# The modulation product of a three-layer kernel, moved from TensorE's gaps to POOL during the gate and up products

## The chip, the core and the metric

The kernel runs on one core of a Trainium2 chip. It is one launch, and the metric is the device time of that launch in microseconds (us). Engines are named as in the profile: PE (TensorE, matmul), PEld (its weight loads), DVE (VectorE), ACT (ScalarE), POOL (GpSimd), SP (SyncE, which only issues transfers here). Each has its own instruction stream, and they meet at semaphores. SBUF is the on-chip memory of 128 partitions, PSUM the banks that matmuls write.

## What is computed

Two hybrid layers (first block), then one layer of a second block. Only the second block has a conditioning vector c, and its modulation is a function of c and of weights alone:

```python
def hybrid_layer(x, ...):                      # called twice
    h = _rms(x) * norm1_g
    proj = h @ w_in
    ...
    o_a = sliding_window_attention(...) @ w_attn_o
    o_b = rwkv7_time_mix(...) @ w_rwkv_o
    o_c = retention(...) @ w_ret_o
    mixed = g[:, :, 0] * o_a + g[:, :, 1] * o_b + g[:, :, 2] * o_c
    x = x + mixed @ w_out
    h2 = _rms(x) * norm2_g
    x = x + (jax.nn.silu(h2 @ w_ffn_gate) * (h2 @ w_ffn_up)) @ w_ffn_down
    return x
# second block: modulation = c @ w_ada + b_ada, (1, 1024) @ (1024, 6144), six vectors of 1024
```

Sizes: 256 tokens, width 1024, hidden width 2816, fp32 throughout. `w_ada` is 25 MB.

## The kernel before

The streams are written out by hand, with no scheduler: what stands in a row in an engine's function is what that engine executes in order. Weights come in slots of 4096 floats a partition through a ring of three (`ring`, SP issues a slot's two transfers of 1 MB as soon as the blocks that read the slot three back are done). PE works in numbered blocks; `Q_...` are block numbers, `S_...` slot numbers, `block_done` counts finished blocks, and `dve_taken` and `act_taken` count the PSUM banks that were emptied.

Most products are split in two parts for precision. ACT copies a weight slot rounded (`high_weights`, L2459), DVE subtracts the copy from the slot (`low_weights`, L2723), and PE multiplies both parts. In the feed-forward part (`ffn`), a slot holds a gate and an up tile of 256 columns; eleven slots follow each other. For a slot, DVE adds the halves of the gate tile (L3139) and the up tile (L3148) from PSUM, multiplies with the silu (L3154), rounds the product (L2751), takes the remainder (L2754), and then makes the low part of the slot two further on (L2723). Block `Q_DOWN`, the first of eight of the down product, follows the last slot.

The modulation product stands in the first block. Each layer handles half of `w_ada`, as six slots of 2 MB (`S_ADA`) in the same ring. `ada(l, n)` on PE multiplies one slot with c: eight matmuls in the code, whose output is 32 partitions wide so that four lie beside each other in the array (L1884). c is a column of `cond`, with zeros around, so that each slot's sum lands in a partition of its own. DVE adds the six results (`ada_rows`, L2918 and L2921) and `ada_columns` turns the sums into columns with four small matmuls (L1893), which DVE adds to the bias in `mod` (L2926).

These six products stand where PE would wait for another engine: one ahead of the two merging levels of the RWKV solve (`rwkv_levels`), two in chunk 0, two in chunk 1 (`rwkv_chunk`), one in the norm and retention part. In the levels, four more gaps hold the four blocks of the first branch's output product (`mix(l, 0, ...)`, L1902), one whole block of 16 recorded matmuls each.

POOL does little: it fills with zeros, multiplies by the cosine table (L1850) and by the retention gate (L1852), and at the layer's end clears semaphores and passes `layer_go` on.

Of the kernel before, what the change touches and what calls it, by code (L numbers as in the profile page):

```python
# [68 lines left out]
LAYER_SLOTS, TWO_SLOTS, EXPERT_SLOTS = 45, 12, 12  # L69
# [12 lines left out]
S_ADA, S_MIX, S_OUT, S_FFN, S_DOWN = [15, 17, 18, 19, 20, 21], [16, 22, 23], 24, 26, 37  # L82
# [3 lines left out]
for _s, _q in list(zip(S_ADA, Q_ADA)) + [(_s, _q[-1]) for _s, _q in zip(S_MIX, Q_MIX)]:  # L86
    SLOT_DONE[_s] = _q + 1
# [178 lines left out]
def build(nc, io):  # L266

    ctx = ExitStack()
    with ctx:
# [30 lines left out]
        mod = sb("mod", [P, 48])  # L300
        bias = sb("bias", [P, 4])
# [116 lines left out]
        mod_rows = w_(15360, 512)  # L418
# [14 lines left out]
        group_sums, group_taken = sem("group_sums"), sem("group_taken")  # L433

# [1344 lines left out]
        def _(sp):  # L1779
# [15 lines left out]
            for l in range(LAYERS):  # L1795
                for n in range(LAYER_SLOTS):
# [32 lines left out]
        def _(pool):  # L1829
            pool.memset(bias[:, 0:1], EPS).then_inc(bias_set, 1)  # L1830
            pool.memset(bias[:, 1:2], LNX_EPS).then_inc(bias_set, 1)
            pool.memset(bias[:, 2:3], 1.0).then_inc(bias_set, 1)
            for l in range(LAYERS):
# [22 lines left out]
                pool.sem_inc(layer_go, 1)  # L1856
            second_pool(pool)

        @block.tensor
        def _(pe):  # L1860
# [15 lines left out]
            def ada(l, n):  # L1876


                q, s = Q_ADA[n], S_ADA[n] % RING
                pe.wait_ge(ring_full[s], full(l, S_ADA[n]))  # L1880
                taken(l, q)
                for k in range(KD):
                    j = 32 * (k % 4)
                    mm = nt.matmul(PS[j:j + 32, bank(l, q), :], cond[:, k, 32 - n:64 - n], ring[:, s, 512 * k:512 * (k + 1)],  # L1884
                                   start=(k < 4), stop=(k >= 4))
                mm.then_inc(block_done, 1)

            def ada_columns(l):

                taken(l, Q_COLS)  # L1890
                pe.wait_ge(dve_taken, taken_at(l, Q_ADA[-1]))
# [1373 lines left out]
```

## Time and profile before

| what | value |
| --- | --- |
| time, median of three runs | 2178.12 us (2176.33 to 2178.39) |
| time of the profiled execution | 2175.79 us |
| its span | 2173.9 us |
| PE busy | 1803.5 us, 83% of the span |
| DVE busy | 941.3 us, 43% |
| ACT busy | 556.0 us, 26% |
| POOL busy | 30.2 us, 1%, 23 instructions |

Times within a trace are in us from the span's start. Layer 0 runs from 0 to about 530 us, layer 1 to about 1040, the second block's mixers to about 1290, and the experts to the end. The profiled execution is 1.9 us longer than its span, and 2.3 us shorter than the median.

### The profile page before, as it was taken

The numbers are of one execution on the slowest core, as the hardware profiler recorded it, in microseconds if no ns is written. First come the engines' busy times: TensorE is split into PE (matmuls) and PEld (weight loads), VectorE is DVE, ScalarE is ACT, GpSimd is POOL, SyncE is SP. The second block draws the span as 40 slices with busy tenths as digits, with TensorE's granted clock in tenths as the row PEclk, the third lists the DMA queues.
The fourth block names the chain that finished last, engine by engine and source line by source line (L and its number), as shares of the span: only waits on it lengthen the run. The fifth ranks groups of instructions, "written<-read, shape, count | busy, mean of one in ns | idle before, by whom it ended". The sixth has DMA issues, their size and how long they took to land.

```text
span 2173.9 us, 31021 instructions
## 1 busy us (share of the span) xinstructions
PE 1803.5 (83%) x13580; PEld 1235.2 (57%) x13580; DVE 941.3 (43%) x1331; ACT 556.0 (26%) x636; POOL 30.2 (1%) x23
## 2 busy tenths in 40 slices
PE   8999999999999999999999987665656566666665
PEld 7998788888999878888878742121111111111111
DVE  7787578666778658765587520000000000000000
ACT  4555023444356212443463020000000000000001
POOL 0000000000000010000000000000000000000000
PEclk9999999999999999999999999887888888887888
DMA  8443645656543364556644689999999999999997
GB/s 288 160 155 131 243 154 173 194 153 215 193 157 128 145 262 142 168 181 168 207 152 156 272 343 427 427 427 429 429 428 428 428 428 429 429 429 428 427 428 320
DMA packets 189606, 613.29 MB, mean 282 GB/s; under 512 B 8344, under 2 KB 105145, under 8 KB 164281
## 3 DMA queue, kind: packets, MB, share of 16 engines
q1 hardware_dynamic: 186928, 602.04, 71.1%
q10 hardware_dynamic: 2568, 9.63, 1.3%
q8 instruction: 88, 1.44, 0.3%
q14 instruction: 22, 0.17, 0.0%
HBM read 610.60 MB, written 1.05 MB: 281 GB/s over the span
## 4 chain that ended last, share of the span: by engine, by line
PE 50%; DMA 37%; DVE 9%; ACT 3%; issue 1%; ACTq 0%; SPq 0%; DVEq 0%; PEldq 0%
DMA work<-in_w_down 13%; DMA work<-in_w_up 12%; DMA work<-in_w_gate 12%; PE PS L1998 10%; PE PS L1999 5%; PE PS L1902 3%; PE PS L1980 3%; PE PS L1973 3%; PE PS L1975 3%; PE PS L1102 3%; PE PS L1866 2%; DVE ring_low L2740 1%; PE PS L794 1%; PE PS L1118 1%; PE PS L2012 1%
## 5 line engine op out<-in xcount | busy, mean ns | idle before, releaser
L1102 PE MATMUL PS<-work,proj 128*32 128x512 f32 x1024 | 155.4, 741 | 98.4 <-DMA work<-in_w_up 59.2
L1704 DVE TENSOR_TENSOR proj<-proj,PS 128x512 f32<-128x512 f32 x16 | 11.0, 687 | 495.4 <-PE PS L1102 495.4
L1998 PE MATMUL PS<-x_both,high_f 128*128 128x512 f32 x608 | 210.9, 396 | 0.0
L1999 PE MATMUL PS<-x_both,ring_low 128*128 128x256 f32 x704 | 195.7, 278 | 0.0
L1102 PE MATMUL PS<-ring,proj 128*32 128x512 f32 x768 | 118.5, 748 | 84.3 <-DMA ring<-in_w_up 46.1
L2723 DVE TENSOR_TENSOR ring_low<-ring,high_f 128x4096 fp32r<-128x4096 f32 (+1 forms) x38 | 146.8, 3863 | 26.6 <-ACT high_f L2459 26.5
L1102 PEld LDWEIGHTS PS<-work,proj 128*32 128x32 f32 x1024 | 31.2, 123 | 216.5 <-DMA work<-in_w_up 96.9
L2459 ACT ACTIVATE high_f<-ring 128x4096 fp32r<-128x4096 f32 (+1 forms) x38 | 121.1, 3187 | 114.3 <-PE PS L1999 96.3
L1395 ACT ACTIVATE proj<-PS 128x512 f32<-128x512 f32 x16 | 9.6, 597 | 515.5 <-PE PS L1102 515.5
L1999 PEld LDWEIGHTS PS<-x_both,ring_low 128*128 128x128 f32 x704 | 132.3, 188 | 0.0
L1708 DVE TENSOR_TENSOR proj<-PS,xT 128x512 f32<-128x512 f32 x32 | 20.7, 686 | 251.5 <-PE PS L1118 234.9
L1998 PEld LDWEIGHTS PS<-x_both,high_f 128*128 128x128 f32 x608 | 114.2, 188 | 26.6
L1102 PEld LDWEIGHTS PS<-ring,proj 128*32 128x32 f32 x768 | 23.6, 123 | 173.5 <-DMA ring<-in_w_up 73.5
L1118 PE MATMUL PS<-work,proj 128*32 128x512 f32 x448 | 74.1, 795 | 48.5 <-DMA work<-in_w_down 45.0
L1998 PE MATMUL PS<-hid_both,high_f 128*128 128x512 f32 x308 | 106.9, 392 | 0.0
L1973 PE MATMUL PS<-xh_a,high_a 128*128 128x256 f32 x384 | 92.9, 283 | 0.0
L1975 PE MATMUL PS<-hT_low,high_a 128*128 128x256 f32 x376 | 91.0, 281 | 0.0
L1397 ACT ACTIVATE proj<-PS 128x512 f32<-128x512 f32 x16 | 9.6, 597 | 300.8 <-PE PS L1110 300.8
L1999 PE MATMUL PS<-hid_both,ring_low 128*128 128x256 f32 x308 | 85.9, 279 | 0.0
L1118 PE MATMUL PS<-ring,proj 128*32 128x512 f32 x352 | 54.0, 743 | 36.7 <-DMA ring<-in_w_down 36.7
L1151 PE MATMUL PS<-proj 128*128 128x512 f32 x128 | 62.6, 632 | 22.8 <-DVE proj L1708 22.8
L1973 PEld LDWEIGHTS PS<-xh_a,high_a 128*128 128x128 f32 x384 | 71.8, 188 | 0.1
(556 smaller groups left out, 3535.6 us busy)
## 6 DMA issues: line engine op xcount, KB each, us to landing
ring<-in_w_in SPq DMA_DIRECT2D x73, 1024.0 KB, 7.2
work<-in_w_gate SPq DMA_DIRECT2D x32, 2048.0 KB, 35.6
work<-in_w_up SPq DMA_DIRECT2D x32, 2048.0 KB, 36.1
work<-in_w_down SPq DMA_DIRECT2D x28, 2048.0 KB, 35.9
ring<-in_w_up SPq DMA_DIRECT2D x25, 2048.0 KB, 35.7
ring<-in_w_gate SPq DMA_DIRECT2D x23, 2048.0 KB, 35.8
ring<-in_w_down SPq DMA_DIRECT2D x22, 2048.0 KB, 36.7
ring<-in_w_ada SPq DMA_DIRECT2D x24, 1024.0 KB, 8.5
```

The source lines that it names most:

```text
L1102: mm = nt.matmul(PS[32 * j:32 * j + 32, 2 + n // 4, :], x(k), w[:, F_E * kk + 512 * j:F_E * kk + 512 * (j + 1)], start=(k == 0), stop=(k = ...
L1118: mm = nt.matmul(PS[32 * c:32 * c + 32, 5 - dh, :], HTE[:, P * c + 32 * d:P * c + 32 * (d + 1)], w(D * c + 512 * dh), start=(d == 0), stop ...
L1151: return nt.matmul(PS[:, YB[2 * t + half], :], GE[:, P * t:P * (t + 1)], (YE, YE2)[half], start=False, stop=False, skip_group_check=True)
L1866: mm = nt.matmul(out[o], weight[:, o], moving, start=start, stop=stop)
L1902: mm = nt.matmul(PS[:, bank(l, q), T * b:T * (b + 1)], weight(b, k), moving(k), start=(k == 0), stop=(k == kn - 1))
L1973: nt.matmul(out, h[:, c:c + P], high_x[:, k, :], start=(k == 0), stop=False)
L1975: nt.matmul(out, h[:, c:c + P], low_x[:, k, :], start=False, stop=False)
L1980: mm = nt.matmul(out, w[:, c:c + P], high_x[:, k, :], start=False, stop=(k == kn - 1 and not late))
L1998: nt.matmul(PS[:, at + b, :], h[:, c:c + P], both[:, k, :], start=(k == 0), stop=False, skip_group_check=True)
L1999: mm = nt.matmul(PS[:, at + b, 0:T], w[:, c:c + P], both[:, k, 0:T], start=False, stop=(k == kn - 1), skip_group_check=True)
L2459: na.activation(high(n)[:, w], ring[:, n % RING, w], ACT.Copy).then_inc(high_ready, 1)
L2723: nv.tensor_tensor(ring_low[:, n % RING, c], w, high(n)[:, c].bitcast(F32), ALU.subtract).then_inc(low_dve, 1)
```

## The change

The modulation is taken out of the ring and off PE's gaps. POOL now loads `w_ada` by its own DMA queue while the layer's gate and up products run, multiplies it by c along the partitions, and adds the eight row blocks. Six sums of 128 x 512 remain per layer; PE sums them over the partitions with six matmuls against a column of ones (`one_row`), in front of `Q_DOWN`. The table of block and slot numbers closes up (39 slots per layer where there were 45). The first branch's four output blocks are cut into eight halves (`mix_half`), which take the places that `ada` had and the four gaps of the levels.

```diff
-Q_ADA = [30, 35, 36, 37, 38, 39]
-Q_MIX = [[31, 32, 33, 34], [41, 42, 43, 44], [45, 46, 47, 48]]
+Q_MIX = [[30, 31, 32, 33], [34, 35, 36, 37], [38, 39, 40, 41]]
-S_ADA, S_MIX, S_OUT, S_FFN, S_DOWN = [15, 17, 18, 19, 20, 21], [16, 22, 23], 24, 26, 37
+S_MIX, S_OUT, S_FFN, S_DOWN = [15, 16, 17], 18, 20, 31
...
+            def in_order(ins):
+                steps[0] += 1
+                ins.then_inc(ada_step, 1)
+                pool.wait_ge(ada_step, steps[0])
+            def modulation(l):
+                w = tri[:, :].rearrange("p (k n) -> p k n", n=512)
+                def part_load(n):
+                    c, k = 512 * (N_ADA * l + n // 2), slice(4 * (n % 2), 4 * (n % 2) + 4)
+                    v = io["w_ada_2"][0][:, c:c + 512].rearrange("(k p) n -> p k n", p=P)
+                    pool.dma_start(w[:, k], v[:, k]).then_inc(ada_full, 16)
+                pool.wait_ge(block_done, done(l, Q_FFN - 1))
+                part_load(0)
+                part_load(1)
+                for n in range(2 * N_ADA):
+                    total, at = ADA_SUMS[n // 2], 4 * (n % 2)
+                    k = slice(at, at + 4)
+                    pool.wait_ge(ada_full, 16 * (2 * N_ADA * l + n + 1))
+                    in_order(pool.tensor_tensor(w[:, k], w[:, k], cond[:, k, 32:33].broadcast_to([P, 4, 512]), ALU.mult))
+                    in_order(pool.tensor_tensor(w[:, at:at + 2], w[:, at:at + 2], w[:, at + 2:at + 4], ALU.add))
+                    if at:
+                        in_order(pool.tensor_tensor(total, total, w[:, at, :], ALU.add))
+                        ins = pool.tensor_tensor(total, total, w[:, at + 1, :], ALU.add)
+                    else:
+                        ins = pool.tensor_tensor(total, w[:, at, :], w[:, at + 1, :], ALU.add)
+                    in_order(ins)
+                    if n + 2 < 2 * N_ADA:
+                        part_load(n + 2)
+                pool.sem_inc(ada_read, 1)
...
                 pool.sem_inc(layer_go, 1)
+                modulation(l)
...
+            def modulation_sums(l):
+                pe.wait_ge(ada_read, l + 1)
+                pe.wait_ge(ada_step, 2)
+                for n in range(N_ADA):
+                    j = 32 * (n % 4)
+                    mm = nt.matmul(PS[j:j + 32, 2, :], one_row[:, 32 - n:64 - n], ADA_SUMS[n], start=(n < 4), stop=(n >= N_ADA - 4))
+                mm.then_inc(ada_rows_ready, 1)
...
             def rwkv_levels(l):
-                ada(l, 0)
+                mix_half(l, 0)
...
-                        i = (lev - BASE_LEVEL) * 2 + pair // 2
-                        mix(l, 0, i, i + 1)
+                        mix_half(l, (lev - BASE_LEVEL) * 2 + pair // 2 + 1)
...
             def rwkv_chunk(l, t):
-                    ada(l, 3)
+                    mix_half(l, 7)
-                    ada(l, 1)
+                    mix_half(l, 5)
-                else:
-                    ada(l, 4)
-                    ada(l, 2)
+                    mix_half(l, 6)
...
                 pe.wait_ge(vr_out, 2)
-                ada(l, 5)
                 scores(4, HEADS)
-                ada_columns(l)
...
+                modulation_sums(l)
                 split_product(l, Q_DOWN, S_DOWN, lambda b, k: P * k, HID_H, HID_low, FB, 1, last_at=11 * l + 10, low_at=11 * l + 11)
+                modulation_columns(l)
```

On DVE, `ada_rows` and `ada_columns` go; one copy of the summed rows and one addition to `mod` come behind `ffn(l)`.

PE around the last gap of the levels and the first of chunk 0. The rows with L1866 (L1908 in the changed kernel) are the solve's own matmuls. Before:

```order
L1866 MATMUL PS<-work,tri 64x64 x16
L1902 MATMUL PS<-proj,ring 128x256 x8
L1866 MATMUL PS<-work,tri 64x64 x32
L1902 MATMUL PS<-proj,ring 128x256 x8
L1866 MATMUL PS<-work,tri 64x64 x16
L1866 MATMUL PS<-work 64x64 x16
L1884 MATMUL PS<-ring,cond 32x512 x8
```

and after:

```order
L1908 MATMUL PS<-work,tri 64x64 x16
L2381 MATMUL PS<-proj,ring 128x256 x4
L1908 MATMUL PS<-work,tri 64x64 x32
L2381 MATMUL PS<-proj,ring 128x256 x4
L1908 MATMUL PS<-work,tri 64x64 x16
L1908 MATMUL PS<-work 64x64 x16
L2381 MATMUL PS<-proj,ring 128x256 x4
```

Each gap holds half an output block where it held a whole one, and a half stands where a modulation slot was multiplied.

POOL behind the end of a layer. L1855 and L1896 are the clearing of the semaphores. Before:

```order
L1852 TENSOR_TENSOR work<-proj 128x1024 [waits oc_out]
L1855 ISA [waits layer_fin]
L1837 MEMSET tri 128x2048 [waits block_done,layer_go]
L1838 MEMSET tri 128x2048
L1841 MEMSET work 128x2048 [waits oa_out]
```

and after (two of twelve parts):

```order
L1893 TENSOR_TENSOR work<-proj 128x1024 [waits oc_out]
L1896 ISA [waits layer_fin]
L1853 DMA tri<-in_w_ada 128x4x512 [waits block_done]
L1853 DMA tri<-in_w_ada 128x4x512
L1862 TENSOR_TENSOR tri<-tri,cond 128x2048 [waits ada_full]
L1863 TENSOR_TENSOR tri<-tri 128x1024 [waits ada_step]
L1868 TENSOR_TENSOR proj<-tri 128x512 [waits ada_step]
L1853 DMA tri<-in_w_ada 128x4x512 [waits ada_step]
L1862 TENSOR_TENSOR tri<-tri,cond 128x2048 [waits ada_full]
L1863 TENSOR_TENSOR tri<-tri 128x1024 [waits ada_step]
L1865 TENSOR_TENSOR proj<-proj,tri 128x512 [waits ada_step]
L1866 TENSOR_TENSOR proj<-proj,tri 128x512 [waits ada_step]
```

POOL gets 42 additions and multiplications and 12 transfers in a layer, each behind the one before.

PE between the last slot of the up product and the down product. Before:

```order
L1998 MATMUL PS<-x_both,high_f 128x512
L1999 MATMUL PS<-x_both,ring_low 128x256
L1973 MATMUL PS<-hid_both,high_f 128x256 [waits dve_taken,high_ready]
L1973 MATMUL PS<-hid_both,high_f 128x256 x17
L1973 MATMUL PS<-hid_both,high_f 128x256 [waits dve_taken]
```

and after:

```order
L2036 MATMUL PS<-x_both,high_f 128x512
L2037 MATMUL PS<-x_both,ring_low 128x256
L1924 MATMUL PS<-proj,one_row 32x512 [waits ada_step,ada_read]
L1924 MATMUL PS<-proj,one_row 32x512 x3
L1924 MATMUL PS<-work,one_row 32x512 x2
L2011 MATMUL PS<-hid_both,high_f 128x256 [waits dve_taken,high_ready]
L2011 MATMUL PS<-hid_both,high_f 128x256 x17
L2011 MATMUL PS<-hid_both,high_f 128x256 [waits dve_taken]
```

The sums over partitions, with their wait for POOL's last addition, have come ahead of `Q_DOWN`.

## Rows read from the trace of the kernel before

**Rows 1.** The page: share of PE busy, in tenths, in 40 slices.

```profile
PE   8999999999999999999999987665656566666665
```

**Rows 2.** Stretches of both layers' gate and up products; columns are in the first row.

```profile
core 0: us, PE busy (x) PEld busy (x) DVE busy (x) ACT busy (x) POOL busy (x), PEclk, DMA share, GB/s
343.50:470.10 126.60, 125.36 (x771) 110.12 (x764) 90.02 (x80) 57.71 (x43) 0.00 (x0) 1.00 0.57 177
864.00:990.60 126.60, 125.36 (x771) 110.16 (x764) 90.02 (x80) 57.71 (x43) 0.00 (x0) 1.00 0.56 173
```

**Rows 3.** Chain of waits, layer 0's solve: start, length, work.

```profile
220.10 1.85 PE PS L1884 x16
...
223.04 3.65 PE PS L1902 x16
...
267.96 1.85 PE PS L1884 x16
```

**Rows 4.** Timeline, ACT and DVE beside those gaps; idle before, and releaser, in brackets.

```profile
222.63 1.28 DVE L2936 TENSOR_TENSOR work<-PS,con 128x512 f32<-128x512 f32 x2
...
268.01 0.60 ACT L2540 ACTIVATE work<-PS 128x512 f32<-128x512 f32 x1 [2.34 <-PE PS L1866]
```

**Rows 5.** Timeline of PE, norm and retention part of layer 0.

```profile
279.97 1.92 PE L1884 MATMUL PS<-ring,cond 128*32 128x512 f32 x16
...
284.52 1.03 PE L1893 MATMUL PS<-con,work 128*128 128x6 f32 x8 [0.36 <-DVE work L2921]
```

**Rows 6.** Timeline of DVE, the same part.

```profile
283.69 0.69 DVE L2921 TENSOR_TENSOR work<-PS,work 128x512 f32<-128x512 f32 x1
284.29 1.94 DVE L3043 TENSOR_TENSOR work<-PS,tri 128x384 f32<-128x384 f32 x4
...
287.78 1.23 DVE L3061 TENSOR_TENSOR work<-work,proj 128x1024 f32<-128x1024 f32 x1
```

**Rows 7.** Timeline of POOL, layer 0: two of its three products.

```profile
252.50 2.37 POOL L1850 TENSOR_TENSOR proj<-proj,con 128x1024 f32<-128x1024 f32 x1 [37.37 <-PE PS L2198]
...
290.42 3.39 POOL L1852 TENSOR_TENSOR work<-proj 128x1024 f32<-128x1024 f32 x1 [21.08 <-ACT proj L2585]
```

**Rows 8.** Timeline of DVE: what ran beside those two.

```profile
252.53 1.23 DVE L3034 TENSOR_TENSOR work<-PS,con 128x1024 f32<-128x1024 f32 x1 [2.35 <-PE PS L2198]
...
290.38 1.23 DVE L3065 TENSOR_TENSOR work<-proj 128x1024 f32<-128x1024 f32 x1 [1.37 <-ACT proj L2585]
```

**Rows 9.** Groups of DVE's instructions, 343.5 to 470.2: busy us, mean ns, idle before.

```profile
L2723 DVE TENSOR_TENSOR ring_low<-ring,high_f 128x4096 fp32r<-128x4096 f32 (+1 forms) x11 | 47.3, 4303 | 7.0 <-ACT high_f L2459 6.9
L2754 DVE TENSOR_TENSOR hid_both<-proj,hid_both 128x512 fp32r<-128x512 f32 x10 | 6.9, 692 | 0.3
L3154 DVE TENSOR_TENSOR proj<-proj 128x512 f32<-128x512 f32 x9 | 6.2, 692 | 0.3
...
L2751 DVE CAST hid_both<-proj 128x512 fp32r<-128x512 f32 x10 | 4.3, 428 | 0.3
L2782 DVE SCALAR_TENSOR_TENSOR hT<-xT,par,work 128x256 f32<-128x256 f32 x8 | 3.2, 479 | 0.0
L2754 DVE TENSOR_TENSOR x_both<-hT,x_both 128x2048 fp32r<-128x2048 f32 x1 | 2.3, 2292 | 0.0
```

**Rows 10.** Timeline of DVE, one slot of the gate and up products, and the next one's low part.

```profile
382.18 0.69 DVE L3148 TENSOR_TENSOR proj<-proj,PS 128x512 f32<-128x512 f32 x1 [2.61 <-ACT proj L2608]
...
385.65 4.43 DVE L2723 TENSOR_TENSOR ring_low<-ring,high_f 128x4096 fp32r<-128x4096 f32 x1 [0.87 <-ACT high_f L2459]
...
396.74 4.42 DVE L2723 TENSOR_TENSOR ring_low<-ring,high_f 128x4096 fp32r<-128x4096 f32 x1 [0.86 <-ACT high_f L2459]
```

**Rows 11.** Timeline: SP's issue as `w_out` ends, and PE's start of `Q_DOWN`.

```profile
343.47 0.37 SPq L1783 DMA_DIRECT2D ring<-in_w_ffn_gate  x1
...
470.03 2.53 PE L1973 MATMUL PS<-hid_both,high_f 128*128 128x256 f32 x20
```

**Rows 12.** The page: a transfer of that size, KB and median us to landing.

```profile
ring<-in_w_ffn_up SPq DMA_DIRECT2D x22, 1024.0 KB, 7.8
```

More of the change, by code:

```diff
@@ L85 @@
     SLOT_DONE[_n] = 2 * _n + 2
-for _s, _q in list(zip(S_ADA, Q_ADA)) + [(_s, _q[-1]) for _s, _q in zip(S_MIX, Q_MIX)]:
+for _s, _q in [(_s, _q[-1]) for _s, _q in zip(S_MIX, Q_MIX)]:
     SLOT_DONE[_s] = _q + 1
@@ L300, in build @@
         mod = sb("mod", [P, 48])
+        one_row = sb("one_row", [P, 64])
         bias = sb("bias", [P, 4])
@@ L415, in first_columns @@
             return slot.rearrange("p (k c) -> p k c", c=512)[:, :, lo:hi]
-        mod_rows = w_(15360, 512)
+        mod_rows = w_(512, 512)
+        ADA_SUMS = [proj[:, b:b + 2, :].rearrange("p a b -> p (a b)") for b in (50, 52, 54, 0)] + [w_(7168, 512), w_(7680, 512)]
         MOD2 = mod[:, :].rearrange("p (l b n) -> p l n b", l=LAYERS, n=4)
@@ L1832, in _ @@
             pool.memset(bias[:, 2:3], 1.0).then_inc(bias_set, 1)
+            pool.memset(one_row[:, :], 0.0).then_inc(ada_step, 1)
+            pool.wait_ge(ada_step, 1)
+            pool.memset(one_row[:, 32:33], 1.0).then_inc(ada_step, 1)
+            steps = [2]
+            def in_order(ins):
[26 more added lines that the diff above has]
+                pool.sem_inc(ada_read, 1)
             for l in range(LAYERS):
@@ L1874, in taken, with modulation_columns @@
                     pe.wait_ge(dve_taken, taken_at(l - 1, LAYER_BLOCKS + q - 2))
[L1876 to L1891, printed above, removed]
+            def modulation_sums(l):
[5 more added lines that the diff above has]
+                mm.then_inc(ada_rows_ready, 1)
+            def modulation_columns(l):
+                pe.wait_ge(ada_rows_out, l + 1)
                 for b in range(4):
-                    mm = nt.matmul(PS[:, bank(l, Q_COLS), N_ADA * b:N_ADA * (b + 1)], mod_rows[:, P * b:P * (b + 1)], con[:, C_SEL:C_SEL + N_ADA],
+                    mm = nt.matmul(PS[:, 3, N_ADA * b:N_ADA * (b + 1)], mod_rows[:, P * b:P * (b + 1)], con[:, C_SEL:C_SEL + N_ADA],
                                    start=True, stop=True)
-                mm.then_inc(block_done, 1)
+                mm.then_inc(ada_cols_ready, 1)
             def product(l, q, weight, moving, kn, n_blocks=2):
@@ L2335, in rwkv_norm_and_retention, with mix_half @@
                 mix(l, 1, 3, 4)
+            def mix_half(l, n):
+                s, i, b = S_MIX[0] % RING, n // 2, n % 2
+                q = Q_MIX[0][i]
+                if n == 0:
+                    pe.wait_ge(oa_out, 3)
+                    pe.wait_ge(ring_full[s], full(l, S_MIX[0]))
+                if b == 0:
+                    taken(l, q)
+                for k in range(HB):
+                    at = D * k + P * n
+                    mm = nt.matmul(PS[:, bank(l, q), T * b:T * (b + 1)], ring[:, s, at:at + P], proj[:, B_AQ + k, :], start=(k == 0), stop=(k == HB - 1))
+                if b:
+                    mm.then_inc(block_done, 1)
             def mix(l, br, lo, hi):
@@ L2912, in rwkv_grams, with modulation_rows, modulation_columns @@
                     nv.copy_predicated(GM[:, h, :], mask, PS[:, 2 + h % 2 + 2 * (h // 2 % 2), 0:3 * P]).then_inc(gram_taken, 1)
-            def ada_rows(l, n):
-                dve.wait_ge(block_done, done(l, Q_ADA[n]))
-                rows = PS[:, bank(l, Q_ADA[n]), :]
-                if n == 0:
-                    nv.tensor_copy(mod_rows[:, :], rows).then_inc(dve_taken, 1)
-                else:
-                    dve.wait_ge(dve_taken, taken_at(l, Q_ADA[n] - 1))
-                    nv.tensor_tensor(mod_rows[:, :], rows, mod_rows[:, :], ALU.add).then_inc(dve_taken, 1)
-            def ada_columns(l):
-                dve.wait_ge(block_done, done(l, Q_COLS))
+            def modulation_rows(l):
+                dve.wait_ge(ada_rows_ready, l + 1)
+                nv.tensor_copy(mod_rows[:, :], PS[:, 2, :]).then_inc(ada_rows_out, 1)
+            def modulation_columns(l):
+                dve.wait_ge(ada_cols_ready, l + 1)
                 m = MOD2[:, l, :, :]
-                nv.tensor_tensor(m, PS[:, bank(l, Q_COLS), 0:4 * N_ADA].rearrange("p (n b) -> p n b", b=N_ADA), m, ALU.add).then_inc(dve_taken, 1)
+                nv.tensor_tensor(m, PS[:, 3, 0:4 * N_ADA].rearrange("p (n b) -> p n b", b=N_ADA), m, ALU.add).then_inc(ada_cols_out, 1)
             def rwkv_levels(l):
-                ada_rows(l, 0)
                 for lev in range(BASE_LEVEL, LEVELS):
```

31 lines of the change are left out of this document (16 added, 15 removed).

## Prediction

> **What bounds the kernel now.** I read the strip of 40 slices first [rows 1]: PE is busy at 0.9 or more through the first block and falls to 0.5 to 0.7 only in the experts, behind everything that the change touches. So in both layers PE's own stream is the length, and a PE instruction less is a gain only where nothing else becomes late. The stretches say it exactly for the gate and up products [rows 2]: 125.36 us of 126.60 are PE busy, at a granted clock of 1.00; DVE is busy 90.02 us, ACT 57.71, POOL nothing. The two layers repeat each other to 0.1 us, so each cost is worked out for layer 0 and doubled. Then I read what stands in PE's gaps of the solve (the chain, [rows 3]), what those gaps cover (timelines, [rows 4 to 6]), and last POOL's few products and what DVE did beside them [rows 7, 8], because the change gives POOL a long job.
>
> **What PE no longer does in the solve.** One `ada` is 1.85 us of the chain and a whole block of the first branch 3.65 us [rows 3]; a half is then 1.83. Before, six `ada` and four blocks: 11.1 + 14.6 = 25.7 us. After, eight halves: 14.6. On paper 11.1 us less. What do the gaps cover?
> - Levels: a gap must cover DVE's two masks, 1.28 us that begin when the first group's matmuls are through and end at 223.91, while PE's gap starts at 223.04 [rows 3, 4]. 0.87 us is needed, a half gives 1.83. All four stay covered.
> - Chunks: three halves of 1.83 stand where `ada` of 1.85 stood. Behind the fourth `ada` of the chunks (267.96) nothing comes in its place. It covered ACT's copy of 0.60 us from 268.01 [rows 3, 4], so PE waits about 0.7 us and gains 1.15 there, not 1.85.
> - Norm and retention: `ada` (from 279.97) and the small column product (1.03 us at 284.52, with a wait of 0.36) go from PE [rows 5]. What is late next is DVE: its rows addition of 0.69 goes, four score products of 1.94 and the two steps up to 287.78 + 1.23 = 289.0 remain in sequence [rows 6], and PE's next output product waits for them. Without 0.69 + 0.19 (the addition to `mod`) and the small wait it comes some 1.2 us earlier, not 3.2.
> Sum: 25.7 less 8 x 1.83 is 11.1, less 0.7 and less 0.65 (1.85 - 1.2): **9.7 us a layer, 19.4 in all.**
>
> **What comes back in front of the down product.** Six matmuls of the form of `ada`'s eight: 6/8 x 1.85 = 1.4, at most 1.85 (four abreast, then two); the column product of 1.03; some 0.2 of waits. DVE's copy (0.7) hides under `Q_DOWN`. **2.6 us a layer, 5.2 in all.** Without anything else the change gives 14.2 us.
>
> **POOL's own work.** Per layer twelve parts: a product of 2048 elements a partition, a sum of 1024, and three additions of 512 for every two parts. That is 12 x 2048 + 12 x 1024 + 18 x 512 = 46,080 elements. POOL's in-place product of 1024 took 2.37 us, the other 3.39 [rows 7]. At 2.37: 106.7 us; at 3.39: 152.5. It begins when `w_out` is done (343.47) plus one transfer of this size, 7.8 us to landing from SP [rows 11, 12], so at 351.3. PE wants the sums at 470.03 [rows 11]. At the low rate, alone, POOL ends at 458 and, with 0.1 us of semaphore between its 42 steps, at 462; POOL's issue of 12 transfers is not in the trace: nothing if it runs beside the work, and if each held POOL as long as SP's queue is held (0.37 us, [rows 11]) 4 us more: 466. **So there are 4 to 8 us of room if nobody disturbs POOL.**
>
> **Who disturbs it.** POOL's two rows differ for a reason that stands beside them. The 2.37 product ran with a DVE instruction that reads one operand from PSUM; the 3.39 product began 0.04 us after a DVE instruction of 1.23 us whose operands both lie in SBUF [rows 8]. The second was longer by 1.02 us, which is most of the 1.19 that DVE still had to run, and DVE's 1.23 did not change. The other layer shows the same pair of figures. I read it as exclusion: POOL stood still while DVE read two SBUF operands.
>
> The Trainium skill (SBUF — State Buffer, in its part on the engine side) says that VectorE and GpSimd share a port pair under "an exclusive lock, not a bandwidth split", taken for a whole instruction by a GpSimd operation that reads SBUF or a VectorE one with two SBUF inputs or in a two-port mode; so far the trace agrees, with its 1.02 us, and it would forbid the overlap that this change counts on. The skill's GPSIMD Engine Reference (elementwise accounting) gives 4497 ns for a sum of 2048 fp32, from which I estimate 101 us for POOL's elements; by that figure, too, the slow row is a disturbed one.
>
> In the gate and up products DVE is mostly of that kind. The groups [rows 9] are 47.3 + 6.9 + 6.2 + 4.3 + 3.2 + 2.3, with two single ones of 1.2 and 0.7 us that repeat L2751 and L3154: 72.1. One 4.4 us low part lies ahead of 351 and goes; the last iteration's 4.9 (0.69 + 0.43 + 0.69 + 3.08) falls behind 470 and comes on top: 72.6. Only the additions from PSUM (L3139, L3148) are free of it. So POOL's 106.7 and DVE's 72.6 stand in one line: 351.3 + 179.3 = **530.6, against 470.0: 60 us late in each layer.** Which side waits hardly matters. If POOL always gives way, PE runs to 470 as before and then stands before `modulation_sums`. If they alternate, DVE's four such instructions of a slot wait behind four of POOL's (106.7/42 = 2.54 us each); a slot has 11.09 us (385.65 to 396.74), its low part ends at 390.1, and PE turns to it at about 392.6 (11.09 behind the end of the slot before, which lies some 0.7 us ahead of 382.18) [rows 10]. With 2.5 us to spare, PE is stretched to 6.2 + 4 x 2.54 = 16.4 us a slot, and the 42 steps last ten slots: the same 55 to 60 us.
>
> Bounds: if POOL goes on at 15% during DVE's instructions (1.02 of 1.19 lost), 72.6 becomes 61.7, and the loss is 50. If handing over costs 0.1 us at each of 42 steps and the transfers' issue 0.37 to 1 us each, it is 60 + 4 + 12 = 76, near the top. I take 60, from the sum without either.
>
> **The sum.** Span 2173.9 - 19.4 + 5.2 + 2 x 60 = 2279.7; with the 1.9 outside the span 2281.6; the median lies 2.3 above the profiled execution: **2284 us, 4.9% slower.** With 50 to 76: 2264 to 2316.
>
> **Rivals.**
> 1. *No exclusion; POOL keeps pace.* The 3.39 row would be due to its operands (it writes elsewhere, L1850 in place). All of POOL's products here but six are in place, so 2.37 holds, POOL ends by 466, and only the 14.2 us count: 2164 us; with a little lateness of up to 5 us a layer, 2174. For it: POOL was idle, only one kind of row speaks against. Against it: 1.02 us beside a 1.23 us instruction, twice, to the hundredth.
> 2. *No exclusion, but POOL is slow.* If 3.39 is POOL's rate for these products, it ends at 351.3 + 152.5 + 4 = 508, 38 us late: 2178 - 14 + 76 = 2240, slower without any lock. It decides from a rate of 2.6 us per 1024.
> 3. *Partial exclusion:* half of DVE's 72.6 blocks, 24 us late: 2212.
> 4. *Transfers in series.* A part's load is issued only when the part two back is finished. If POOL's queue took long or the transfers did not overlap with its work, up to 12 x 7.8 = 94 us a layer would come on top. PE's weights take 177 GB/s in this stretch [rows 2], so room is there; against it. Some of it would give 2320 and more.
>
> **How the numbers follow.** Chances: exclusion, 60 us (50 to 76) a layer, 0.66; rival 2, 0.06; rival 3, 0.08; rival 4, 0.05; rival 1, 0.15. The likeliest gives 2284. The range 2225 to 2320 takes in the first, rival 2 and a part of rival 3, about 0.77; it leaves out rival 1. A measurement of this kernel can tell 0.2% (4.4 us) from nothing. Rival 1 is faster except for its late end: faster 0.13, same 0.03, slower 0.84.
>
> **What would show it.** In the profile after: POOL's 2048-element products of 4.7 us alone, but 5 to 9 us beside L2723's successor; or DVE's low part at 5 to 9 us where it was 4.43. PE idle before the `one_row` matmuls, or before the gate and up tiles with a DVE low part as releaser; slots longer than 11.09 us. The gate and up stretch at about 187 us instead of 126.6, and the solve 9.7 us shorter a layer. I would be wrong if POOL's products stayed near 4.7 us and DVE's at 4.43 side by side, or if the two overlapped less because the waits of one fell into the idle time of the other.

## The result, and the profile after

| | median us | runs, us | profiled span, us |
|---|---|---|---|
| before | 2177.93 | 2176.33 to 2178.39 (4) | 2173.9 |
| after | 2254.43 | 2246.78 to 2257.2 (4) | 2245.0 |

The ratio is 1.035, with a 95% interval of 1.0332 to 1.0367: the change makes the kernel 3.5% slower. 76 us were lost where I had forecast 106.

The page of the profile after, first its engines' busy time, then the slices and the chain that answer to [rows 1]:

```profile
PE 1818.9 (81%) x13412; PEld 1249.1 (56%) x13412; DVE 1059.2 (47%) x1321; ACT 554.2 (25%) x636; POOL 318.2 (14%) x133
...
PE   8999996989999999689999998656666666666665
...
POOL 0000008970000010897000000000000000000000
PEclk9999997999999999899999999887878878788877
...
PE 41%; DMA 35%; DVE 19%; ACT 3%; issue 2%; ACTq 0%; SPq 0%; DVEq 0%; PEldq 0%
```

POOL's two blocks of work (8, 9, 7) are the products of the two layers. In the first slice of each, PE falls to 6 and its granted clock to 7 and 8. DVE has ten instructions fewer than before, yet is busy for 1059 us. It was busy for 941, so at least 118 us of its "busy" time is not work.

Layer 0 in four stretches of the kernel after: the solve, the part from norm and retention to the end of `w_out`, gate and up, the down product and the start of the next layer. The columns are the length, the busy time and (count) of PE, PEld, DVE, ACT and POOL, the granted clock, the DMA share and the rate.

```profile
204.90:279.70 74.80, 71.72 (x927) 59.17 (x926) 44.87 (x79) 9.71 (x18) 7.63 (x5) 1.00 0.23 84
279.70:335.00 55.30, 53.65 (x321) 46.65 (x320) 41.76 (x53) 12.23 (x6) 3.39 (x1) 1.00 0.35 115
335.00:502.50 167.50, 136.54 (x774) 118.68 (x770) 151.87 (x80) 56.68 (x43) 143.91 (x54) 0.90 0.66 209
502.50:560.00 57.50, 57.50 (x357) 50.35 (x358) 36.88 (x42) 18.43 (x8) 0.00 (x0) 1.00 0.68 188
```

The solve and the part behind it end 9 us earlier in the layer than before: the `w_out` blocks end 130.1 us after the solve's start, where it had been 139.0 (204.5 to 343.5). The gate and up stretch takes 167.5 us where it took 126.6 [rows 2]. PE was idle in it for 31.0 us (167.5 less 136.5), and its own busy time grew from 125.4 to 136.5, at a clock of 0.90 instead of 1.00. One layer is therefore 41 - 9 us longer, plus some 5 us in front of and behind the down product. From POOL's filling of `tri` with zeros in layer 0 to the same step in layer 1 it is 558.3 us, against 521.1 before: 37.2 more. In layer 1 the gate and up stretch is some 39 us longer, and the whole span 71.1 us.

What TensorE waited for in that stretch (us in total, times, the longest):

```profile
PE PS L2011 <- DVE x_both L2803: 14.9, 1, 14.9
PE PS L2036 <- DVE proj L3181: 12.2, 5, 4.6
PE PS L2023 <- DVE x_both L2806: 2.3, 1, 2.3
```

These and the smaller ones are all waits for DVE. There is none for POOL, which had finished by 494.1, 8 us before PE wanted the sums.

DVE and POOL side by side, layer 0. First DVE behind the second norm and in a later slot, in the kernel after; these rows answer to [rows 10]:

```profile
345.24 17.93 DVE L2834 SCALAR_TENSOR_TENSOR hT<-xT,par,work 128x256 f32<-128x256 f32 x8
363.20 1.23 DVE L2803 CAST x_both<-hT 128x2048 fp32r<-128x2048 f32 x1
364.47 6.07 DVE L2806 TENSOR_TENSOR x_both<-hT,x_both 128x2048 fp32r<-128x2048 f32 x1
...
402.08 4.41 DVE L2775 TENSOR_TENSOR ring_low<-ring,high_f 128x4096 fp32r<-128x4096 f32 x1
406.42 0.67 DVE L3181 TENSOR_TENSOR proj<-proj,PS 128x512 f32<-128x512 f32 x1
408.35 0.69 DVE L3190 TENSOR_TENSOR proj<-proj,PS 128x512 f32<-128x512 f32 x1 [1.25 <-ACT proj L2660]
409.07 1.45 DVE L3196 TENSOR_TENSOR proj<-proj 128x512 f32<-128x512 f32 x1
410.55 2.51 DVE L2803 CAST hid_both<-proj 128x512 fp32r<-128x512 f32 x1
413.10 1.67 DVE L2806 TENSOR_TENSOR hid_both<-proj,hid_both 128x512 fp32r<-128x512 f32 x1
414.69 5.50 DVE L2775 TENSOR_TENSOR ring_low<-ring,high_f 128x4096 fp32r<-128x4096 f32 x1
```

And POOL at the same times:

```profile
345.20 3.62 POOL L1862 TENSOR_TENSOR tri<-tri,cond 128x2048 f32<-128x2048 f32 x1
348.90 2.44 POOL L1863 TENSOR_TENSOR tri<-tri 128x1024 f32<-128x1024 f32 x1
351.42 1.33 POOL L1868 TENSOR_TENSOR proj<-tri 128x512 f32<-128x512 f32 x1
...
402.01 0.79 POOL L1853 DMA_DIRECT2D tri<-in_w_ada  x1 [0.40 <-POOL proj L1868]
402.83 7.14 POOL L1862 TENSOR_TENSOR tri<-tri,cond 128x2048 f32<-128x2048 f32 x1
410.04 2.73 POOL L1863 TENSOR_TENSOR tri<-tri 128x1024 f32<-128x1024 f32 x1
412.86 1.36 POOL L1865 TENSOR_TENSOR proj<-proj,tri 128x512 f32<-128x512 f32 x1
414.29 1.62 POOL L1866 TENSOR_TENSOR proj<-proj,tri 128x512 f32<-128x512 f32 x1
```

The two lists can be read against each other to within 0.15 us. DVE's low part runs from 402.08 to 406.49 at its usual 4.41. POOL's product begins at 402.83 and is through at 409.97, 3.5 us behind the end of the low part (alone it takes 3.62): 7.14 in all. The record of DVE's L3196 begins at 409.07, but it ends at 410.52, 0.55 us behind that product, and so takes 1.45 instead of 0.69. Then POOL's sum of 1024 waits for L3196 (2.73 for 2.41), the cast behind L3196 waits for that sum (2.51 for 0.43), and so on. The two engines take turns, one instruction each, and the side that waits shows its waiting as busy time. Only the additions that read one operand from PSUM (0.67 to 0.69) are as long as ever. The eight small instructions of the norm, 3.25 us together in the kernel before, took 17.93: seven of them waited, each for one of POOL's, and one (0.47) fell into POOL's pause between two parts. POOL's steps beside them took 3.62, 2.44 and 1.33 us, as long as alone.

### The profile page after: what moved, and what is told of

Same layout as the page of the kernel before. It is cut to its first block, busy times and chain, and to the rows that moved or that the text cites. A ratio compares the mean times of both kernels' runs of the same rounds, so it can differ in the third digit from the quotient of the medians.

```text
span 2245.0 us, 30737 instructions
## 1 busy us (share of the span) xinstructions
PE 1818.9 (81%) x13412; PEld 1249.1 (56%) x13412; DVE 1059.2 (47%) x1321; ACT 554.2 (25%) x636; POOL 318.2 (14%) x133
## 3 DMA queue, kind: packets, MB, share of 16 engines
HBM read 610.60 MB, written 1.05 MB: 272 GB/s over the span
## 4 chain that ended last, share of the span: by engine, by line
PE 41%; DMA 35%; DVE 19%; ACT 3%; issue 2%; ACTq 0%; SPq 0%; DVEq 0%; PEldq 0%
DMA work<-in_w_down 8%; DMA work<-in_w_up 7%; DMA work<-in_w_gate 6%; PE PS L2036 5%; DMA ring<-in_w_down 5%; DMA ring<-in_w_gate 5%; DVE ring_low L2775 5%; DMA ring<-in_w_up 3%; PE PS L1105 3%; PE PS L2011 3%; PE PS L2018 3%; PE PS L2013 3%; PE PS L2037 2%; PE PS L1940 2%; DVE hid_both L2803 2%
## 5 line engine op out<-in xcount | busy, mean ns | idle before, releaser
L2036 PE MATMUL PS<-x_both,high_f 128*128 128x512 f32 x608 | 221.5, 408 | 26.7 <-DVE proj L3181 24.0
L2775 DVE TENSOR_TENSOR ring_low<-ring,high_f 128x4096 fp32r<-128x4096 f32 (+1 forms) x38 | 167.6, 4409 | 11.0 <-ACT high_f L2511 10.9
L2037 PEld LDWEIGHTS PS<-x_both,ring_low 128*128 128x128 f32 x704 | 136.5, 194 | 0.0
L1862 POOL TENSOR_TENSOR tri<-tri,cond 128x2048 f32<-128x2048 f32 x24 | 133.2, 5549 | 0.6
L1154 PE MATMUL PS<-proj 128*128 128x512 f32 x128 | 69.4, 690 | 22.8 <-DVE proj L1711 22.8
```

The costliest lines, as they stand in the source:

```text
L1154: return nt.matmul(PS[:, YB[2 * t + half], :], GE[:, P * t:P * (t + 1)], (YE, YE2)[half], start=False, stop=False, skip_group_check=True)
L1862: in_order(pool.tensor_tensor(w[:, k], w[:, k], cond[:, k, 32:33].broadcast_to([P, 4, 512]), ALU.mult))
L2036: nt.matmul(PS[:, at + b, :], h[:, c:c + P], both[:, k, :], start=(k == 0), stop=False, skip_group_check=True)
L2037: mm = nt.matmul(PS[:, at + b, 0:T], w[:, c:c + P], both[:, k, 0:T], start=False, stop=(k == kn - 1), skip_group_check=True)
L2775: nv.tensor_tensor(ring_low[:, n % RING, c], w, high(n)[:, c].bitcast(F32), ALU.subtract).then_inc(low_dve, 1)
```

## Experiments

All are edits of the kernel after. "Stretch" is layer 0's time from the end of its `w_out` blocks to the first matmul of the sums (before: of `Q_DOWN`), 126.6 us before and 167.7 after (0.2 more than above, since its two ends are set a little wider), and PE's and DVE's busy times and the clock are those of the stretch. The ratios of e1 to e7 are to runs of the kernel before that were made beside each experiment (medians 2176.2 and 2176.1 us), so they are not quite the quotients of the second column.

| | median us | ratio to before | stretch | PE | DVE | clock | PE waits for POOL |
|---|---|---|---|---|---|---|---|
| before | 2177.93 | 1 | 126.6 | 125.4 | 90.0 | 1.00 | - |
| after | 2254.43 | 1.035 | 167.7 | 136.7 | 152.2 | 0.90 | 0 |
| e1, no product | 2166.44 | 0.995 | 127.0 | 125.7 | 90.4 | 1.00 | 0 |
| e2, transfers only | 2170.58 | 0.9979 | 130.4 | 126.3 | 90.4 | 1.00 | 0 |
| e3, writes only | 2191.47 | 1.0074 | 137.7 | 126.8 | 102.7 | 0.98 | 9.1 |
| e4, late start | 2248.6 | 1.033 | 167.4 | 132.5 | 149.4 | 0.92 | 19.7 |
| e5, half of it | 2226.09 | 1.0226 | 155.8 | 132.9 | 126.8 | 0.92 | 0 |
| e6, fine pieces | 2284.66 | 1.05 | 185.2 | 129.2 | 136.3 | 0.88 | 43.6 |
| e7, on DVE | 2166.29 | 0.9948 | 127.8 | 125.7 | 121.7 | 1.00 | 0 (DVE 0.9) |

**e1: without the product.**

```diff
-                part_load(0)
-                part_load(1)
-                for n in range(2 * N_ADA):
-                    ... (product, sums, next load)
+                for total in ADA_SUMS[:]:
+                    in_order(pool.memset(total, 0.0))
```

> POOL does neither the twelve transfers nor the arithmetic of the product; it only sets the six totals to zero, so the second block is computed without its modulation. Everything else stands as in the changed kernel. Theory (POOL's arithmetic and DVE keep one another out of SBUF): the whole loss goes with the arithmetic, and what is left is the front's gain of 9 us a layer less some 3 to 5 us for the sums and columns ahead of the down product: 2164 to 2170 us, solve and gate-and-up stretch 75.7 and 126.6 us. Rival (the order of TensorE's work or the moved half tiles cost something of their own in the gate and up products): over 2178.

Measured: 2166.44 us, ratio 0.995 (0.9933 to 0.9966), the stretch back at 127.0. PE's reordering costs nothing in the gate and up products, and the whole loss of 88 us (2254.4 - 2166.4) comes from what POOL does for the product. The rest of the change is a gain of 0.5%.

**e2: the transfers, but no arithmetic.**

```diff
+                for n in range(2 * N_ADA):
+                    if n > 1:
+                        pool.wait_ge(ada_full, 16 * (2 * N_ADA * l + n - 1))
+                    part_load(n)
+                pool.wait_ge(ada_full, 16 * 2 * N_ADA * (l + 1))
```

The six totals are set to zero as in e1.

> POOL issues all twelve transfers of a layer and waits for each, but does no arithmetic (the totals are zero, so the modulation is left out). Theory (port): as without any of it, within 3 us, so 2164 to 2172; two transfers stay under way at a time, and if the second one again begins to land 8 us late, that has nothing to do with the arithmetic. Rival (the 6.3 MB a layer take bandwidth from the weight slots, which then come late): 2190 to 2250, with TensorE waiting for ring slots in the gate and up products.

Measured: 2170.58 us, ratio 0.9979 (0.9969 to 0.9988). So the 12.6 MB a layer (twelve transfers of 1 MB; the 6.3 MB of the expectation is half of it) cost 4 us in all, most of it one wait of 2.8 us in layer 0's stretch. The rate in the stretch went from 177 to 269 GB/s. POOL's second transfer again stood at the head of its queue (POOL, e2):

```profile
338.36 0.92 POOL L1853 DMA_DIRECT2D tri<-in_w_ada  x1 [0.31 <-POOL work L1857]
345.90 0.76 POOL L1853 DMA_DIRECT2D tri<-in_w_ada  x1 [6.62 <-issue]
351.80 0.75 POOL L1853 DMA_DIRECT2D tri<-in_w_ada  x1 [5.14 <-DMA tri<-in_w_ada]
```

Without any arithmetic it still went out 6.6 us behind the end of the first issue. The landing times in the trace say what it stood for: the first transfer landed at 345.58, and the second was issued at 345.90. All eleven later issues of layer 0 in e2 came 0.30 to 0.31 us behind the landing of the transfer before, the third too, whose semaphore asks only for the first transfer. So one transfer of POOL's was under way at a time and not two, against the expectation, and the twelve took 101 us (338.4 to 439.7). In the kernel after the second issue came 8.45 us behind the end of the first and 0.32 behind its landing (344.11), and since POOL's program has both loads ahead of the first product, the product began at 345.2, 10.2 us into the stretch.

**e3: POOL as busy, but only writing.**

```diff
-                    in_order(pool.tensor_tensor(w[:, k], w[:, k], cond[...].broadcast_to([P, 4, 512]), ALU.mult))
-                    in_order(pool.tensor_tensor(w[:, at:at + 2], w[:, at:at + 2], w[:, at + 2:at + 4], ALU.add))
+                    for _ in range(2):
+                        in_order(pool.memset(w[:, k], 0.0))
+                    for _ in range(3):
+                        in_order(pool.memset(w[:, at:at + 2], 0.0))
```

and three memsets of 512 for each of the additions into the totals.

> The transfers stay. Each product of 2048 becomes two memsets of 2048 on the same buffer (2 x 1.82 us for 3.62), each sum of 1024 three memsets of 1024, each sum of 512 three of 512: about 106 us of POOL a layer, in the same order and between the same semaphores, but nothing is read (the modulation comes out zero and so is left out). Theory (the two engines keep one another out only where POOL reads SBUF): DVE's low part is back at 4.4 us and the time at 2164 to 2175, although POOL is as busy as in the changed kernel. Rival (any work of POOL in SBUF does it, or POOL's semaphores and transfers): 2240 to 2260, like the changed kernel. Between the two, the share of the loss that writing alone brings.

Measured: 2191.47 us, 21 above e2, and between the two forecasts. Its waits of PE say where the 21 come from (layer 0 the first row; layer 1 has 10.1):

```profile
PE PS L1931 <- POOLq L1879: 9.1, 1, 9.1
PE PS L2018 <- DVE x_both L2810: 0.7, 1, 0.7
```

9.1 + 10.1 = 19.2 us are simply POOL being late: the memsets and the steps between them came to 127 us a layer, from 345.05 to 472.0, more than I had planned. Most of DVE's waiting is gone: in the stretch its low parts average 4423 ns, its products and remainders of 512 elements 692 ns and the norm's eight 477 ns, as in e1. A slot of e3 on DVE, and POOL in the same time:

```profile
397.39 0.69 DVE L3203 TENSOR_TENSOR proj<-proj 128x512 f32<-128x512 f32 x1
398.11 2.37 DVE L2810 CAST hid_both<-proj 128x512 fp32r<-128x512 f32 x1
400.52 0.69 DVE L2813 TENSOR_TENSOR hid_both<-proj,hid_both 128x512 fp32r<-128x512 f32 x1
401.13 4.42 DVE L2782 TENSOR_TENSOR ring_low<-ring,high_f 128x4096 fp32r<-128x4096 f32 x1
```

```profile
398.38 3.86 POOL L1863 MEMSET tri<- 128x2048 f32 x2
402.30 2.98 POOL L1865 MEMSET tri<- 128x1024 f32 x3
```

The low part (4.42) and the two-operand steps (0.69) run at full pace through POOL's memsets, and POOL's memsets of 1024 at theirs (2.98 for three). **So DVE's instructions with two SBUF operands are kept out by a POOL instruction that reads SBUF, and not by one that only writes it.** One kind still waits. The cast takes 0.43 us where POOL is not in its way and 2.37 here, until 0.2 us behind the end of the first memset of 2048 (398.38 + 1.9), though its record begins 0.27 us ahead of the memset's. It averages 1094 ns over the whole of e3 and 427 ns in e7's stretch. It is the only one of a slot's instructions that moves 512 elements in under 0.5 us. The waiting goes the other way too: beside the cast of 128x2048 (348.19 to 349.84) three memsets of 1024 took 3.94 us where they take 2.98.

No run has the arithmetic without the transfers. That the two have to come together is not ruled out by a run of its own, but the rows above show DVE waiting for POOL's arithmetic instructions one by one.

The Trainium skill (SBUF — State Buffer, the part on the engine side) says just this: the lock on the shared port pair is taken by any GpSimd instruction against a VectorE one in a two-port mode, and by a reading one alone against a VectorE one with two SBUF inputs. e3 agrees on both, with its 2.37 and its 4.42 us, if the cast runs in such a mode, which its 0.43 us suggests and no row says.

**e4: POOL's arithmetic begins behind the norm's small instructions.**

```diff
                 part_load(0)
                 part_load(1)
+                pool.wait_ge(h_ready, 11 * l + 9)
```

> POOL issues its first two transfers as in the changed kernel but begins its arithmetic only when the norm's last eight small instructions on DVE are done (some 15 us later); nothing is left out. Theory A (the time both engines need of the port is what counts, wherever it lies): 2245 to 2262, the idle time of TensorE ahead of the first gate product goes and comes back in the slots or ahead of the sums, since POOL had only 8 us of slack there. Theory B (the loss is that idle time of TensorE, 15 us a layer, behind small DVE instructions that each waited for one of POOL's, and the slots' stretch is bounded by POOL's rate anyway): 2222 to 2230.

Measured: 2248.6 us, ratio 1.033, within theory A's range and far from B's. It is 6 us below the median of the kernel after, inside the spread of that kernel's own runs (2246.8 to 2257.2), and its stretch is 0.3 us shorter. PE's wait of 14.9 us ahead of the first gate product is gone (0.2), and this stands in its place, ahead of the sums:

```profile
PE PS L1925 <- POOLq L1873: 19.7, 1, 19.7
```

POOL began 7 us later (352.2; not 15, since the norm's eight instructions were no longer held up) and ended 8 us later (502.1). PE's waits for DVE in the slots came to 13.9 us. One wait was exchanged for another, and moving the start gains nothing that can be told from noise.

**e5: half of the product.**

```diff
-                for n in range(2 * N_ADA):
+                for n in range(N_ADA):
...
-                    if n + 2 < 2 * N_ADA:
+                    if n + 2 < N_ADA:
```

The other three totals are set to zero.

> POOL makes three of a layer's six column groups; the other three totals are zero, so half of the modulation is left out. That is half of POOL's 96 us of arithmetic. Theory A (what costs is that DVE waits for POOL, and TensorE for DVE, as long as POOL works): the 15 us ahead of the first gate product stay, and some four slots of 2.4 us more: 25 of the 41 us a layer, so 2210 to 2220. Theory B (only the sum of both engines' port time against the length of the stretch counts): 48 + 73 us fit between 345 and 470, so nothing is lost but what the slots' slack can't hide: 2168 to 2180. A loss in proportion would be 2207 to 2212.

Measured: 2226.09 us, ratio 1.0226 (1.0211 to 1.0242), above all three forecasts, theory A's 2210 to 2220 too. Half of the work costs two thirds of the loss: the stretch is 28.8 us longer than e1's, not 20. Theory B, by which only the sum against the stretch's length counts, falls: 48 + 73 us would have fitted. What the waits show is that PE has nothing to do while DVE waits, and its waits come at once, with the first product (14.5 us ahead of the first gate tile, then 5.8 + 1.8). Ten-microsecond windows of e5 show what that does to TensorE beside the waiting:

```profile
345.00:355.00 10.00, 4.89 (x42) 4.69 (x40) 10.00 (x7) 4.25 (x2) 8.20 (x5) 0.93 0.77 244
355.00:365.00 10.00, 0.60 (x3) 0.60 (x4) 9.93 (x5) 0.00 (x0) 9.74 (x5) 0.50 0.56 192
365.00:375.00 10.00, 10.00 (x60) 9.74 (x60) 9.90 (x5) 0.60 (x1) 9.42 (x5) 0.72 0.31 105
375.00:385.00 10.00, 8.24 (x48) 6.97 (x47) 9.93 (x5) 4.12 (x2) 9.50 (x4) 1.00 0.77 258
```

PE was idle for 9.4 of the 10 us from 355, its granted clock went down to 0.50 (1.2 GHz), and it stayed low for a part of the next window, where PE was busy throughout. Of the 28.8 us, 7.2 are PE's busy time (132.9 against 125.7) and 21.6 its idle time. In the kernel after it is 11.0 and 29.7.

**e6: pieces of 512.**

```diff
-                    in_order(pool.tensor_tensor(w[:, k], w[:, k], cond[...].broadcast_to([P, 4, 512]), ALU.mult))
+                    for i in range(at, at + 4):
+                        in_order(pool.tensor_tensor(w[:, i], w[:, i], cond[:, i, 32:33].broadcast_to([P, 512]), ALU.mult))
```

and the sum of 1024 as two of 512.

> Nothing is left out; each product of 2048 is cut into four of 512 and each sum of 1024 into two of 512, so POOL has 90 steps a layer instead of 42, and DVE waits for a piece of under 1 us where it waited for one of up to 3.6. Theory A (port time in sum decides): DVE's eight small instructions take 8 to 9 us instead of 17.9 and the slots are shorter, but POOL gets on more slowly and TensorE waits for it ahead of the sums: 2245 to 2265, as in the changed kernel. Theory B (the size of the pieces that DVE waits for decides): 2205 to 2225.

Measured: 2284.66 us, ratio 1.05, worse than either forecast, and slower than the kernel after by 30 us. The sign is theory A's. DVE waits less: its busy time in the stretch is 45.9 us above e1's instead of 61.8 (136.3 and 152.2 less 90.4), some 6 of the 45.9 are the last slot's instructions, which fall inside this longer stretch, and the norm's eight take 9.7 us instead of 17.9. But now POOL waits at nearly each turn for whatever DVE has, and one of those turns is the low part (POOL, e6):

```profile
400.04 1.62 POOL L1867 TENSOR_TENSOR proj<-proj,tri 128x512 f32<-128x512 f32 x1
401.74 5.34 POOL L1868 TENSOR_TENSOR proj<-proj,tri 128x512 f32<-128x512 f32 x1
...
408.30 5.15 POOL L1863 TENSOR_TENSOR tri<-tri,cond 128x512 f32<-128x512 f32 x4
```

The addition of 5.34 takes 1.26 to 1.32 alone. Four products of 512 take 4.41 to 4.61 us alone where one of 2048 took 3.62, and POOL needs 174 us (345.0 to 519.4) for what took it 149. Of these 25 us some 10 are the pieces' own price (12 x 4.41 + 12 x 2.60 + 18 x 1.26 = 106.8 us alone, against 96.3); the rest is waiting. PE stands for 43.6 us ahead of the sums.

**e7: the product on DVE itself.**

```diff
+ADA_STEPS = [(0, 0)] + [(4, 1)] * 9 + [(3, 0)]
+ADA_LOADS = [4, 4, 6, 8, 11, 13, 16, 18, 21, 23, 24]
...
-                modulation(l)
...
+                        for p in range(lo, hi):
+                            if p >= 4:
+                                sp.wait_ge(ada_used, 8 * N_ADA * l + 2 * (p - 4) + 2)
+                            ...
+                            sp.dma_start(ADA_W[:, k], v[:, k]).then_inc(ada_full[p % 4], 16)
...
+                    if k:
+                        ins = nv.scalar_tensor_tensor(total, ADA_W[:, k, :], cond[:, k, 32:33], total, ALU.mult, ALU.add)
+                    else:
+                        ins = nv.tensor_scalar(total, ADA_W[:, k, :], cond[:, k, 32:33], None, ALU.mult)
+                    ins.then_inc(ada_used, 1)
...
                         nv.tensor_tensor(silu, silu, halves(l, Q_FFN + 2 * n)[1], ALU.add).then_inc(dve_taken, 1)
+                    ada_steps(l, ADA_STEPS[n][0])
...
+                    ada_steps(l, ADA_STEPS[n][1])
                     low_weights(l, S_FFN + 2 + n)
```

> Nothing is left out: the product goes to DVE, as 48 multiply-and-add instructions of 512 a layer (four behind the addition of each gate and up slot, one ahead of the low part, three in the last slot), its columns loaded by SP in pieces of two row blocks behind the slots' weights. POOL is idle. Theory (port time decides): 48 x about 0.65 = 31 us a layer stand beside DVE's 73 in a stretch of 126 us, where POOL's 96 did not fit: 2162 to 2176, the front's gain kept. Rival (DVE's holes of some 3 us a slot are too small or lie in the wrong place, so TensorE waits for hidden tiles in each slot): 2180 to 2215.

Measured: 2166.29 us (2163.12 to 2166.98), ratio to before 0.9948 (0.9934 to 0.9961): **0.5% faster than before, 3.9% faster than the change as made.** It is as fast as the kernel without any product. The stretch takes 127.8 us, PE is busy in it for 125.7 at a clock of 1.00, and of its waits 0.9 us is for DVE's last step. The groups of DVE's instructions in that stretch of layer 0:

```profile
L2749 DVE TENSOR_TENSOR ring_low<-ring,high_f 128x4096 fp32r<-128x4096 f32 x10 | 44.2, 4420 | 0.3 <-ACT high_f L2485 0.2
L3162 DVE SCALAR_TENSOR_TENSOR proj<-tri,cond,proj 128x512 f32<-128x512 f32 x28 | 21.0, 750 | 1.3 <-DMA tri<-in_w_ada 0.3
L3162 DVE SCALAR_TENSOR_TENSOR work<-tri,cond,work 128x512 f32<-128x512 f32 x14 | 10.5, 750 | 1.1 <-DMA tri<-in_w_ada 0.6
...
L3164 DVE TENSOR_SCALAR proj<-tri,cond 128x512 f32<-128x512 f32 x4 | 1.9, 483 | 1.4 <-DMA tri<-in_w_ada 1.4
```

The same product is 48 instructions and 34.4 us (21.0 + 10.5 + 1.9, and two more of 0.48) on DVE, where multiply and add are one instruction, and 96.3 us on POOL, counted at its undisturbed durations. DVE was busy for 90.4 of 127.0 us (e1) and is now for 121.7 of 127.8. It fits, just: idle is 6 us.

## Why the prediction came out as it did

**The likeliest case was the right one, and its size was too large.** Exclusion was forecast at 0.66, on the two pairs of [rows 7, 8]; e1 to e3 show it. But it was given 50 to 76 us a layer, 2264 to 2316 in all, and 41 us and 2254 lie below that. The measured time falls into 2225 to 2320 only because that range was widened for two rivals that did not come true. The mechanism was right; that the range held is in part luck. Rival 1, no exclusion at 2164 to 2174, tells what the change would have been worth: e1 and e7 measure 2166. Rivals 2 and 3 have no support. POOL's sums of 1024 take 2.41 alone, and its addition of 512 that writes elsewhere takes 1.33, as the ones in place do (1.32), so the 3.39 row was a disturbed one. And where a two-operand instruction of DVE met POOL's arithmetic, one of the two was held, not in half of the cases. Of rival 4 the premise came true, one transfer at a time, but not its price: 4 us for all transfers in e2, and in the kernel after each had landed before POOL wanted it.

**The front: right.** Forecast 9.7 us a layer, measured 9.0 (75.7 us from the solve's start to the first matmul of the next output product, against 84.7). The wait forecast where the fourth `ada` of the chunks is gone is there too, as PE's wait for ACT's `work`, 0.7 us.

**Sums and columns: right, with a term missed.** Forecast 2.6. In e1 it is 10.5 us from the end of the gate and up tiles to the second set of down tiles, against 8.3 before: 2.2. What I did not count comes behind it. PE arrives at the next layer some 6 us earlier, and the transfer of that layer's first slot does not come earlier by as much: ACT's copy waits for it, DVE's low part for the copy, and DVE's first step for PE stands behind the low part. So PE waits 1.7 us (e7, ACT and PE):

```profile
520.51 3.65 ACT L2485 ACTIVATE high<-ring 128x4096 fp32r<-128x4096 f32 x1 [6.51 <-DMA ring<-in_w_in]
529.85 0.38 PE L1952 MATMUL PS<-xu_h,high 128*128 128x256 f32 x1 [1.66 <-DVE xu_h L2789]
```

**POOL's work: a term mis-sized.** I took 2.37 us per 1024 elements from [rows 7] for all 46,080, 106.7 us in all. Its longest piece came out at 3.62 for 2048, not 4.74; the 1024 sum at 2.41 and the 512 ones at 1.33. That is 12 x 3.62 + 12 x 2.41 + 18 x 1.33 = 96.3 us. The 2.37 row was a product with a table of cosines, each value another one. In the new product the second operand is one value for 512 elements; its rate of 1.8 us per 1024 no row of before showed. The figure of the Trainium skill (GPSIMD Engine Reference, 4497 ns for a sum of 2048), from which I had estimated 101 us, fits the sum of 1024 (2.41) better than this product.

**The sum of both: the step that failed.** I put POOL's 106.7 and DVE's 72.6 in one line, 179.3 us from 351.3 to 530.6, and had PE wait for its end. POOL's span was 149 us (345.2 to 494.1), and PE was at the sums 8.3 us behind its end. The 30 us between 179 and 149 are:
- 10.4: POOL's arithmetic, above.
- some 9: DVE had 64 us of such work within POOL's span, not 72.6 (nine low parts of 4.42, ten casts of 0.43, nine each of the steps of 0.69, and the norm's 7.5). The last slot came behind it, and is in the 8.3.
- some 11 left: 96 + 64 is still more than 149. Of this, 4.3 are the slots' ten casts, which POOL holds up but which hardly hold POOL up (its addition of 1.36 beside the end of a cast, where alone it takes 1.33), and 3.2 the norm's eight instructions, beside which POOL went on at full pace. The rest, some 4, I can't place row by row; an overlap of about 0.1 us at each turn (3.5 us behind the low part's end for a product of 3.62) would be of that size.

Against that stand 2.4 us by which POOL began later in the stretch than forecast (10.2 us instead of 7.8), for the second transfer, and the 8.3. So 60 - 30 + 2.4 + 8.3 = 41, the measured loss.

**"Which side waits hardly matters": half right.** e4 moves 15 us from one side to the other, and the stretch stays as it is (167.4 and 167.7). But e5 loses 28.8 us for half of POOL's work and e6 loses 58 for all of it in smaller pieces, against 41. Wherever DVE is made to wait, PE does so soon after; where POOL waits, only its end counts. And the clock was not in the sum at all: 11 of the 41 us are growth of PE's own busy time (136.7 against 125.7). Much of that is TensorE at 1.2 GHz behind its idle times, as two windows of the kernel after show:

```profile
365.00:375.00 10.00, 7.68 (x36) 7.38 (x35) 9.90 (x5) 0.00 (x0) 9.44 (x4) 0.50 0.32 105
385.00:395.00 10.00, 10.00 (x60) 8.73 (x59) 9.41 (x5) 3.27 (x3) 9.42 (x5) 1.00 1.01 344
```

36 matmuls take 7.68 us at a granted clock of 0.50, where 60 take 10.00 at 1.00.

**The description of the profile after** was right in its signs: products of 5 to 9 us (6.5 to 7.1), a low part of 5 to 9 (5.5 to 8.2 in some slots, 4.4 in others), most slots 12.6 to 13.7 us long instead of 11.09, PE waiting for a DVE step. I had expected slots of 16.4, with four full waits each. The low part and the steps before it often met a POOL instruction that was nearly done, or its 1.2 us between two parts (0.40 of idle time, 0.79 of issue), in which DVE's two-operand instructions ran at full pace (the start of the low part at 402.08).

## What to carry to other kernels

Idle time on POOL was not free capacity here while DVE worked on SBUF operands: add the SBUF-reading time of both, set it against the stretch, and count the waits on DVE first if the bound engine waits for DVE. Before work is moved to POOL, ask what the same work takes on DVE, since SBUF is read either way: here 34 us in DVE's own holes instead of 96 on POOL. Cutting POOL's pieces smaller made it worse: the pieces cost more of their own, and POOL waited at more of its turns.

## What the runs showed that I had not expected

- A DVE cast at double pace (0.43 us for 128x512) is held up even by a memset on POOL (2.37 us), while instructions with two SBUF operands are not (e3).
- A POOL product whose second operand is one value for 512 elements takes 3.62 us for 128x2048, less than two products of 1024 with the cosines (2 x 2.37).
- POOL's transfers went one at a time: the second was issued 8.45 us behind the first in the kernel after and 6.6 us with no arithmetic anywhere on POOL (e2), each time some 0.3 us behind the landing of the first, and so it was for all twelve in e2. What in POOL's queue makes it so is open; no run changed the queue.
- The memsets cost POOL more than planned: 127 us for 106, of which 10 x 0.76 us is the issue of the transfers, and the rest idle time between steps and a few waits for DVE's casts. So e3 alone, without the list of waits, would have read as a partial exclusion.
